# Hybrid decoder step: the feed-forward projections as two-by-two block products with seven products

## The chip, the cores and the metric

One core of a Trainium2 chip runs the whole program once. The metric is the device time of one execution in microseconds (us). TensorE multiplies, VectorE (DVE), ScalarE (ACT) and GpSimd (POOL) work on elements, SyncE (SP) only issues DMAs. SBUF is the on-chip memory with 128 partitions, PSUM has 8 banks into which TensorE writes, HBM is the memory outside.

## The reference

One layer of a decoder: a prompt of 1024 tokens and a sample group of 32 tokens share all weights, so T = 1056 columns. Three token mixers and their merge come first. The change touches what follows them:

```
x = x + (mixed @ w_out)
h2 = rmsnorm(x, norm2_w)
gu = h2 @ w_ffn_up                                   # 1024 -> 2 x 2816
x = x + (silu(gu[..., :D_FF]) * gu[..., D_FF:]) @ w_ffn_down   # 2816 -> 1024
y = rmsnorm(x, norm_f)                               # final norm
```

All in fp32.

## The kernel before

**Layout.** Activations lie with the feature on the partition and the token on the column: X1 is [128, 8, 1056], eight feature blocks (k = 0 to 7). The columns are cut in three chunks of 384, 384 and 288 (CHUNKS), because a PSUM bank holds 512 columns.

**Precision.** Each product of two fp32 numbers is made of three matmuls: every operand is split in a high part (rounded to fp32r) and a low part (the rest), and mm3 (lines 1277 to 1279) adds high weight x low data, low weight x high data and high weight x high data in PSUM. Each of the three has its own load of 128 x 128 weights.

**Weights.** A unit is 128 x 1024 weights, one output tile of a projection with depth 8 (or less for the down projection). SP loads it raw into WRAW (line 867), POOL loads it a second time into WH as the high part (the DMA into an fp32r tile, line 958) and subtracts to get the low part WL (line 961). There are two slots for each.

**FFN.** The 22 blocks of the inner width (2816 / 128) are cut in four passes of 6, 6, 5 and 5 blocks (FFN_PASSES). In a pass, each block needs two up tiles (gate and value). ACT takes Silu of the gate tile (line 2306), DVE multiplies (line 2355, FM), ACT casts the high part FH (line 2311) and DVE subtracts to the low part FL. FH and FL stay in SBUF. Then 8 down tiles of that pass, with depth 6 or 5, are added to X1 by DVE (add_to_x1). The loops over up and down tiles run in hardware loops on TensorE, SP and POOL. first_pair("up0") runs two up tiles interleaved, since it follows the norm's splitting chunk by chunk, and last_pair reorders the last two tiles of "out" and "down3" by chunk, so that the norm of a chunk can start early.

**Norms.** The norm ahead of the FFN (number 2) scales X1 into six small buffers HF5 (line 769), ACT casts them to HH (line 782), DVE and POOL subtract to HL (lines 755 and 1143). The final norm (number 3) works on single columns: TensorE sums the squares with a matmul of one column (lines 714 and 722), ACT takes the root and DVE the reciprocal of 2 or 3 columns (lines 676 and 702), TensorE spreads them (line 732), and DVE and POOL scale the rows, which SP and ACT store (lines 945 and 1844).

**Order.** Each engine runs its own instructions in the written order. Semaphores say what is ready: acc_done and acc_free for PSUM tiles, split_ok for weights, h_lo and f_lo for low parts. DMAs of one queue are also served in the order of issue.

## Time and profile before

| | us |
|---|---|
| median of three runs | 1761.59 (1761.56 to 1764.63) |
| span of the profiled execution | 1761.2 |
| TensorE busy | 1736.7 |
| DVE, ACT, POOL busy | 681.7, 384.9, 501.6 |
| FFN up to its last matmul, from the third up tile | 743.95 |

The profile is of one execution. A matmul's duration in it overlaps the next one's; the distance between two starts is what a matmul takes of the engine. PE is TensorE, PEld its weight loads. A time in a row's first column counts from the span's start. The shape of a matmul is rows x columns of the weights, then partitions x columns of the moving data.

### The profile page before, as it was taken

Reading aid. Unit: us, or ns where it says so; the run is one execution under the profiler, and the core shown is the slowest. Engines: PE = TensorE matmul, PEld = TensorE weight load, DVE = VectorE, ACT = ScalarE, POOL = GpSimd, SP = SyncE. Lnnn points to the kernel's source line nnn. Section 1 sums busy time; section 2 is a strip of 40 time slices with the busy share of each in tenths; the row PEclk is TensorE's granted clock in tenths of the full one; section 3 lists DMA queues with packets and bytes.
Section 4 is the critical chain, followed back from the end, with each engine's and each line's share of the span. In section 5 each row is a group of like instructions: output and inputs, shape, how many; then the busy total and the mean of one; then the engine's idle time right before and its main releaser. Section 6 shows DMA issues by size and latency. Waiting matters only on the chain.

```text
span 1761.2 us, 28504 instructions
## 1 busy us (share of the span) xinstructions
PE 1736.7 (99%) x11497; PEld 1689.1 (96%) x11497; DVE 681.7 (39%) x1406; ACT 384.9 (22%) x937; POOL 501.6 (28%) x504
## 2 busy tenths in 40 slices
PE   7999999999999999999999999999999999999998
PEld 7999999999999998898999999999999999999997
DVE  6859611318245537778732611110112111111125
ACT  5331121332123323534110411001110011001121
POOL 5482122223221211313223322222222222232222
PEclk9999999999999999999999999999999999999999
DMA  5454452332332345343642222233222322233224
GB/s 199 88 129 131 124 185 86 98 88 84 96 94 93 122 125 172 98 149 119 219 158 95 84 84 84 81 98 96 95 81 87 108 84 91 75 109 96 79 75 136
DMA packets 78384, 193.39 MB, mean 110 GB/s; under 512 B 13504, under 2 KB 33216, under 8 KB 78040
## 3 DMA queue, kind: packets, MB, share of 16 engines
q1 hardware_dynamic: 45616, 89.54, 16.7%
q0 software_dynamic: 20624, 66.10, 12.4%
q10 hardware_dynamic: 12056, 36.54, 6.0%
q8 instruction: 59, 0.97, 0.2%
q14 instruction: 29, 0.24, 0.0%
HBM read 167.45 MB, written 24.48 MB: 109 GB/s over the span
## 4 chain that ended last, share of the span: by engine, by line
PE 92%; DVE 4%; issue 1%; ACT 1%; DMA 1%; POOL 0%; SPq 0%; DVEq 0%; ACTq 0%; POOLq 0%
PE ps L1277 29%; PE ps L1278 28%; PE ps L1279 28%; PE ps L1707 1%; PE ps L1798 1%; PE ps L1477 1%; PE ps L1451 1%; ACT SB L2164 1%; PE ps L1771 0%; PE ps L1471 0%; PE ps L1652 0%; PE ps L1420 0%; DVE W_im L2355 0%; PE ps L1594 0%; DVE KTS L2355 0%
## 5 line engine op out<-in xcount | busy, mean ns | idle before, releaser
L1277 PE MATMUL ps<-HL,WH 128*128 128x384 f32 (+1 forms) x2496 | 819.0, 328 | 5.1 <-DVE HL L625 1.8
L1278 PE MATMUL ps<-HH,WL 128*128 128x384 f32 (+1 forms) x2496 | 807.0, 323 | 0.0
L1279 PE MATMUL ps<-HH,WH 128*128 128x384 f32 (+1 forms) x2496 | 805.9, 323 | 0.0
L1277 PEld LDWEIGHTS ps<-HL,WH 128*128 128x128 f32 x2496 | 469.5, 188 | 16.6 <-issue 9.3
L1278 PEld LDWEIGHTS ps<-HH,WL 128*128 128x128 f32 x2496 | 469.9, 188 | 0.3
L1279 PEld LDWEIGHTS ps<-HH,WH 128*128 128x128 f32 x2496 | 469.6, 188 | 0.0
L961 POOL TENSOR_TENSOR WL<-WRAW,WH 128x1024 fp32r<-128x1024 f32 (+2 forms) x131 | 295.0, 2252 | 449.3 <-DMA WH<-in_w 449.3
L958 POOL DMA_DIRECT2D WH<-in_w x131 | 75.5, 576 | 689.3 <-PE ps L1279 679.6
L2355 DVE TENSOR_TENSOR FM<-FS,ps 128x384 f32<-128x384 f32 (+1 forms) x66 | 34.3, 520 | 435.5 <-PE ps L1279 431.6
L1278 PE MATMUL ps<-FH,WL 128*128 128x384 f32 (+1 forms) x528 | 170.6, 323 | 0.0
L1277 PE MATMUL ps<-FL,WH 128*128 128x384 f32 (+1 forms) x528 | 169.9, 322 | 0.2 <-POOL WL L961 0.2
L1279 PE MATMUL ps<-FH,WH 128*128 128x384 f32 (+1 forms) x528 | 169.8, 322 | 0.0
L2355 DVE TENSOR_TENSOR X<-X,ps 128x384 f32<-128x384 f32 (+1 forms) x108 | 56.2, 521 | 233.3 <-PE ps L1279 233.3
L2306 ACT ACTIVATE FS<-ps 128x384 f32<-128x384 f32 (+1 forms) x66 | 30.6, 465 | 402.0 <-PE ps L1279 402.0
L1277 PEld LDWEIGHTS ps<-FL,WH 128*128 128x128 f32 x528 | 99.2, 188 | 0.5 <-POOL WL L961 0.5
L1279 PEld LDWEIGHTS ps<-FH,WH 128*128 128x128 f32 x528 | 99.2, 188 | 0.0
L1278 PEld LDWEIGHTS ps<-FH,WL 128*128 128x128 f32 x528 | 99.1, 188 | 0.0
L2311 ACT CAST FH<-FM 128x384 fp32r<-128x384 f32 (+1 forms) x66 | 31.9, 487 | 224.1 <-DVE FM L2355 224.1
L1867 ACT ACTIVATE GT<-ps 128x384 f32<-128x384 f32 (+1 forms) x72 | 33.3, 464 | 214.1 <-PE ps L1279 187.9
L2363 DVE SCALAR_TENSOR_TENSOR CV<-PX,CW,CV 128x120 f32<-128x120 f32 (+9 forms) x90 | 45.8, 575 | 0.6
L2363 DVE SCALAR_TENSOR_TENSOR PX<-PX,ps 128x384 f32<-128x384 f32 (+1 forms) x60 | 30.9, 517 | 23.0 <-PE ps L1279 16.0
L1853 ACT COPY PX<-ps 128x384 f32<-128x384 f32 (+1 forms) x36 | 16.3, 453 | 96.3 <-PE ps L1279 95.1
(361 smaller groups left out, 1610.7 us busy)
## 6 DMA issues: line engine op xcount, KB each, us to landing
WRAW<-in_w SPq DMA_DIRECT2D x111, 512.0 KB, 3.3
WH<-in_w POOLq DMA_DIRECT2D x102, 512.0 KB, 3.7
gate_scratch<-GT ACTq DMA_DIRECT2D x24, 528.0 KB, 3.2
PX<-gate_scratch ACTq DMA_DIRECT2D x22, 528.0 KB, 3.8
WRAW<-in_w SPq DMA_DIRECT2D x16, 384.0 KB, 3.0
WH<-in_w POOLq DMA_DIRECT2D x16, 384.0 KB, 3.3
WRAW<-in_w SPq DMA_DIRECT2D x16, 320.0 KB, 2.8
WH<-in_w POOLq DMA_DIRECT2D x16, 320.0 KB, 3.1
```

The lines of the kernel that those rows point to most:

```text
L958: nc.gpsimd.dma_start(WH[:, slot, 0:wd], src[:, 0:wd]).then_inc(s_high[slot], 16)
L961: nc.gpsimd.tensor_tensor(WL[:, slot, 0:wd], WRAW[:, slot, 0:wd], WH[:, slot, 0:wd].bitcast(F32), ALU.subtract).then_inc(split_ok, 1)
L1277: nc.tensor.matmul(out, wh, rl, start=start, stop=False)
L1278: nc.tensor.matmul(out, wl, rh, start=False, stop=False)
L1279: return nc.tensor.matmul(out, wh, rh, start=False, stop=stop)
L1451: last = nc.tensor.matmul(o[64 * e:64 * e + 64], STT[:, part, pr, 64 * e:64 * e + 64], U[:, 2 * pr + e, 0:SC], start=True, stop=True)
L1477: last = nc.tensor.matmul(o(i, e), off[r:r + 64, pr, :], HST[r:r + 64, part, 2 * half + i, :], start=False, stop=part == 1, skip_group_che ...
L1867: nc.scalar.activation(GT[:, c0:c0 + w], acc_of(no, n)[:, 0:w], ACT.Tanh, scale=0.5).then_inc(acc_free[n], 1)
L2306: nc.scalar.activation(FS[:, n, 0:w], acc[n][:, 0:w], ACT.Silu).then_inc(acc_free[n], 1)
L2311: nc.scalar.copy(FH[:, f, c0:c0 + w], FM[:, n, 0:w]).then_inc(f_hi, 1)
L2355: return nc.vector.tensor_tensor(out, a, b, op)
L2363: return nc.vector.scalar_tensor_tensor(out=out, in0=a, scalar=s, in1=b, op0=op0, op1=op1)
```

## The change

**The algorithm.** The moving data (h with 1024 features x 1056 tokens) is seen as two by two blocks: features 0 to 511 and 512 to 1023, tokens 0 to 527 (LOWER) and 528 to 1055 (UPPER). The weights of a pair of output tiles are also two by two blocks. Seven products of sums of blocks replace eight products of blocks. A product covers one block row of outputs: 128 outputs, half the tokens in two pieces of 264 columns (CHUNK), depth 4 in the up part. A group x is one pair of output tiles: seven products in the order 1, 5, 6, 7, 3, 2, 4. Their results are combined in PSUM and by DVE: products 6, 3 and 4 add onto the banks of products 1, 5 and 7 (QUAD, FRESH), after ACT has copied product 1 (R1) and then product 6 (R2) out; DVE adds quadrants from them.

**Up part.** The first block's two up tiles stay as they were. 21 groups (UP_PAIRS) do the other 42 tiles. Before the first, DVE forms four sums of h blocks in X1, in place, ACT casts their high parts and DVE subtracts the low parts; X1 itself has been stored in HBM (xscr), and the norm scales X1 in place where it used HF5. POOL forms four differences of weight blocks per group, in place in the raw weights, and seven low parts. The high parts of the weights are now copied by ACT, not loaded by DMA; a ring of six slots of 512 weights (RING) holds high and low.

**Between.** Of each pair of inner blocks, seven rows (four blocks' halves and three sums, high and low) are made by DVE and ACT and stored in HBM (fscr), ten pairs beside the up groups, the eleventh beside the first down groups.

**Down part.** Four stages over the inner width with 4, 6, 6 and 6 blocks (DOWN_TILES), depth 2, 3, 3, 3 in a product; each has four groups, one per pair of output tiles. SP loads each stage's rows from fscr and X1 back from xscr. DVE adds nine results per group to X1.

**Final norm.** Sums of squares, root and reciprocal are taken on the spread array, 128 partitions wide and 528 columns long, once for each half of the tokens.

All loops of the FFN are now written out. The core of the diff:

```diff
+HALF = T // 2
+CHUNK = HALF // 2
+UP_PAIRS = DFF // P - 1
+DOWN_TILES = [4, 6, 6, 6]
+PAIRS = UP_PAIRS + 4 * len(DOWN_TILES)
+ORDER, LAST_ORDER = (1, 5, 6, 7, 3, 2, 4), (1, 5, 6, 7, 4, 3, 2)
+QUAD = {1: 0, 6: 0, 5: 2, 3: 2, 7: 4, 4: 4, 2: 6}
+FRESH = (1, 5, 7, 2)
+RING = 6
...
# norm 2 on DVE: in place, behind the stores of X1
-            dve.scalar_tensor_tensor(m["hf"][i % slots][:, 0:w], m["src"](k)[:, c0:c0 + w], prm(m["weight"], k, 1),
+            if i == 0:
+                after(dve, s_x1s, 16 * LATE[0])
+            if k == LATE[0]:
+                after(dve, s_x1c[n], 16)
+            dve.scalar_tensor_tensor(m["src"](k)[:, c0:c0 + w], m["src"](k)[:, c0:c0 + w], prm(m["weight"], k, 1),
...
# POOL
+        for x in range(PAIRS):
+            after(pool, s_wr[x % 2], raw_loaded(x))
+            low(x, 0)
+            difference(x, W12, W11, W11, 1, 0)
+            difference(x, W22, W12, W12, 1, 1)
+            low(x, 1)
+            difference(x, W22, W11, W11, 2, 2)
+            low(x, 2)
+            difference(x, W21, W11, W11, 3, 3)
+            for i in range(3, 7):
+                low(x, i)
...
# TensorE
+            product, nk, g = order_of(x)[i], depth(x), 7 * x + i
+            bank_free(x, product)
+            after(pe, wl_ok, g + 1)
+            high, lo = ring(g)
+            for c in range(2):
+                out = quad(product)[:, c, :]
+                for k in range(nk):
+                    mh, ml = moving(x, product, k, c)
+                    wh, wl = high[:, k * P:(k + 1) * P], lo[:, k * P:(k + 1) * P]
+                    nc.tensor.matmul(out, wh, ml, start=product in FRESH and k == 0, stop=False, skip_group_check=True)
+                    nc.tensor.matmul(out, wl, mh, start=False, stop=False, skip_group_check=True)
+                    last = nc.tensor.matmul(out, wh, mh, start=False, stop=k == nk - 1, skip_group_check=True)
+            last.then_inc(pd.sem, 1)
...
# TensorE's waits in the first group (x = 0)
+                for n, tiles in {1: ((0, 1), (1, 1)), 5: ((2, 1), (0, 2)), 7: ((1, 2), (2, 2))}.get(product, ()):
+                    pe.wait_ge(acc_free[n], FFN_TILE + tiles)
+                if product == 6:
+                    after(pe, ar_used, 1)
...
# ACT, the first group (the norm's splitting stands just ahead)
+        weight_high(0)
+        first_silu(0)
+        h_sum_high(0)
+        weight_high(1)
+        first_silu(1)
+        h_sum_high(1)
+        weight_high(2)
+        weight_high(3)
+        h_sum_high(2)
+        first_silu(2)
+        for x in range(UP_PAIRS):
+            g, q = 7 * x, f_pair_beside(x)
+            if x >= 1:
+                silu(x - 1, RV, 5)
+            weight_high(g + 4)
+            if x == 0:
+                h_sum_high(3)
+            after(act, pd, done_count(x, 1))
...
+            nc.scalar.copy(by_chunk(R1), quad(1)).then_inc(ar_used.sem, 1)
...
# DVE, the first group
+        first_product(0)
+        h_sum(A22, A21, A22, ALU.add, 0)
+        h_sum_low(0)
+        first_product(1)
+        h_sum(A21, A11, A21, ALU.subtract, 1)
+        h_sum(A11, A22, A11, ALU.subtract, 2)
+        h_sum_low(1)
+        first_product(2)
+        h_sum_low(2)
+        h_sum(A12, A12, A11, ALU.subtract, 3)
+        h_sum_low(3)
...
# SP, last up group: x1_load and f_load are row loads of [128, 1056]
+                for s in range(STAGE):
+                    after(sp, s_fst[s], 16 * len(range(s, 70, STAGE)))
+                for j in range(2, 6):
+                    x1_load(j)
+                f_load(0, 0, done_count(x, 5))
+                f_load(0, 1)
+            raw_load(x + 2)
+            if x == UP_PAIRS - 1:
+                f_load(0, 2, done_count(x, 6))
+                f_load(0, 3)
+                f_load(0, 4, done_count(x, 7))
+                f_load(0, 5)
+                f_load(0, 6, done_count(x, 4))
...
# final norm on DVE
+            sums = quad((1, 7)[i])
+            dve.reciprocal(sums, sums).then_inc(frc.sem, 1)
```

## Rows read from the trace of the kernel before

**Rows 1.** The page: busy shares, granted clock, the chain that ended last.
```profile
PE 1736.7 (99%) x11497; PEld 1689.1 (96%) x11497; DVE 681.7 (39%) x1406; ACT 384.9 (22%) x937; POOL 501.6 (28%) x504
PE 92%; DVE 4%; issue 1%; ACT 1%; DMA 1%; POOL 0%; SPq 0%; DVEq 0%; ACTq 0%; POOLq 0%
```

**Rows 2.** Busy time by stretch (start:end, length, engines, clock, DMA share, GB/s).
```profile
1004.95:1748.90 743.95, 743.76 (x4630) 743.44 (x4629) 121.63 (x240) 74.48 (x147) 192.89 (x146) 1.00 0.28 88
```

**Rows 3.** Timeline of TensorE in an up tile: start, duration, line, operands, shape.
```profile
1205.12 0.34 PE L1278 MATMUL ps<-HH,WL 128*128 128x384 f32 x1
...
1210.04 0.34 PE L1279 MATMUL ps<-HH,WH 128*128 128x384 f32 x1
1210.21 0.29 PE L1277 MATMUL ps<-HL,WH 128*128 128x288 f32 x1
...
1211.94 0.29 PE L1278 MATMUL ps<-HH,WL 128*128 128x288 f32 x1
```

**Rows 4.** Timeline: loads and matmuls of few columns.
```profile
975.40 0.75 PEld L722 LDWEIGHTS ps<-PRM,AC 128*128 128x128 f32 x6
180.71 1.06 PEld L1471 LDWEIGHTS ps<-U,KTS 128*128 128x128 f32 x8
180.89 1.09 PE L1471 MATMUL ps<-U,KTS 128*128 128x137 f32 x8
```

**Rows 5.** Timeline from the norm's first scaling to the third up tile.
```profile
960.88 0.33 SPq L867 DMA_DIRECT2D WRAW<-in_w  x1
976.66 1.11 DVE L769 SCALAR_TENSOR_TENSOR FS<-X,PRM,ps 128x384 f32<-128x384 f32 x2
999.42 0.43 ACT L782 CAST HH<-FM 128x288 fp32r<-128x288 f32 x1 [0.36 <-DVE FM L769]
999.89 0.46 DVE L755 TENSOR_TENSOR HL<-FM,HH 128x288 fp32r<-128x288 f32 x1 [0.50 <-ACT HH L782]
1000.02 1.28 ACT L2306 ACT_TABLE_LOAD   x1 [0.16 <-POOL HL L1143]
1004.95 0.34 PE L1277 MATMUL ps<-HL,WH 128*128 128x384 f32 x1
```

**Rows 6.** Groups by form (count, busy us, mean ns), and one timeline row.
```profile
L2355 DVE TENSOR_TENSOR FL<-FM,FH 128x384 fp32r<-128x384 f32 x44 | 22.4, 551 | 0.0
L522 DVE TENSOR_TENSOR AC<-AC,GT 128x1056 f32<-128x1056 f32 x6 | 7.5, 1254 | 0.2
1213.98 1.39 DVE L2355 TENSOR_TENSOR FL<-FM,FH 128x384 fp32r<-128x384 f32 x3
L1898 ACT CAST WH<-WRAW 128x512 fp32r<-128x512 f32 x4 | 2.3, 611 | 0.5 <-DMA WRAW<-in_w 0.5
L1172 POOL TENSOR_TENSOR WL<-WRAW,WH 128x512 fp32r<-128x512 f32 x4 | 4.9, 1275 | 0.0
L986 POOL TENSOR_TENSOR HST<-BC,SP 128x256 f32<-128x256 f32 x4 | 2.7, 696 | 0.1
```

**Rows 7.** Timeline of TensorE after its idle start.
```profile
17.36 0.69 PE L1277 MATMUL ps<-HL,WH 128*128 128x384 f32 x1 [1.81 <-DVE HL L625]
22.65 0.41 PE L1278 MATMUL ps<-HH,WL 128*128 128x384 f32 x1
```

**Rows 8.** A stretch with busy DMAs; a DMA issue (KB, us to landing).
```profile
4.00:24.00 20.00, 13.40 (x52) 12.09 (x53) 12.81 (x25) 13.43 (x29) 15.25 (x22) 1.00 1.05 385
WRAW<-in_w SPq DMA_DIRECT2D x111, 512.0 KB, 3.3
```

**Rows 9.** Timeline of the end.
```profile
1748.64 0.29 PE L1279 MATMUL ps<-FH,WH 128*128 128x288 f32 x1
1752.56 4.71 DVE L2363 SCALAR_TENSOR_TENSOR X<-X,PRM,ps 128x384 f32<-128x384 f32 x10
```

**Rows 10.** Reciprocals by form.
```profile
L2389 DVE RECIPROCAL SP<-SP 128x16 f32<-128x16 f32 x1 | 0.2, 221 | 0.0
L340 DVE RECIPROCAL DTT<-DTT 128x72 f32<-128x72 f32 x1 | 0.6, 603 | 0.0
```

More of the change, by code:

```diff
@@ new lines, in _, with final_sum @@
+        for x in range(PAIRS - 1):
+            for i in range(7):
+                strassen_product(x, i)
+        def final_sum(product, half, squares, start, stop):
+            for c in range(2):
+                last = nc.tensor.matmul(quad(product)[:, c, :], prm("ones"), by_chunk(squares[:, half])[:, c, :], start=start,
+                                        stop=stop, skip_group_check=True)
+            return last
+        for i in range(6):
+            strassen_product(PAIRS - 1, i)
@@ new lines, in _, with quadrant @@
+        first_product(0)
[9 more added lines that the diff above has]
+        h_sum_low(3)
+        def quadrant(x, out, held, product, turn):
+            after(dve, pd, done_count(x, product))
+            tt(by_chunk(out), by_chunk(held), quad(product), ALU.add).then_inc(dr.sem, 1)
```

649 lines of the change are left out of this document (509 added, 140 removed).

## The prediction

> **What bounds the kernel now.** The page's busy shares come first: TensorE is busy for 1736.7 of 1761.2 us, DVE, ACT and POOL for under half, and the chain that ended last lies on TensorE for 92% [rows 1]. The stretches of the feed-forward part (FFN) come second: from its third up tile to its last matmul there are 743.95 us, TensorE is busy for 743.76 of them, the granted clock is 1.00 (the 2.4 GHz level), DVE and POOL have 122 and 193 us of work and the DMAs run at 88 GB/s [rows 2]. So here a matmul less is time less, until another engine or a transfer is late. Third is the timeline: what a matmul costs is the distance of two starts, not its duration of 0.34 us, which overlaps. 28 steps of 384 columns take 4.92 us (175.7 ns each), 13 steps of 288 columns 1.73 us (133.1 ns) [rows 3]. An up tile is 48 of the first and 24 of the second, 11.63 us; the waits between tiles cost nothing.
>
> **The matmuls.** The first up pair stays. Before, the other 42 up tiles and the 8 x 22 down steps take the 743.95 us. After, each of 21 pairs is 7 products x 2 halves x 4 steps x 3 = 168 matmuls, and the down part 4 x 7 x 2 x 3 x 11 = 1848 (11 is the sum of the depths 2, 3, 3, 3): 5376 matmuls of 264 columns. Columns fall by one eighth, which at before's rate would be 93 us. But no matmul of 264 columns with full weights is in the trace. From 288 to 384 columns a start costs 0.444 ns per column more, and the line gives 133.1 - 24 x 0.444 = 122.4 ns at 264. The other side is the weight load, one per matmul as before: six loads with one-column matmuls take 0.75 us, (0.75 - 0.19)/5 = 112 ns each, and eight with 137 columns (1.06 - 0.19)/7 = 124 ns by the loads, (1.09 - 0.28)/7 = 116 ns by the matmuls [rows 4]. The ends are thus 112 ns (only the load binds) and 133 ns (no fall below the 288 step); if the step bends between 137 and 288 columns, the chord gives 116 + 127/151 x 17 = 130 ns. I take 123 ns, the line, rounded up: 264 columns are nearest to the 288 row and the load still fits. 5376 x 0.123 = 661.2 us; the small matmuls among the last tiles (four groups of six, each near the 0.7 us of [rows 4]) give way to one of about 0.25 us. The stretch becomes 661.5 us: **-82.5 us**.
>
> The Trainium skill, page "TensorE: Matmul & The Clock Gate", section "Back-to-back issue gap", gives N/2.4 + 2.5 ns for an isolated warm matmul. By it, an estimate, a step of 264 columns is 112.5 ns and the matmuls 605 us, 56 us less than my term; but at 288 it says 122.5 where this trace has 133.1, and at 384 it says 162.5 where the trace has 175.7, so I go by the trace.
>
> **The start of the block products.** Before, DVE and ACT end the norm's splitting at 1000.3 and 999.85, and TensorE goes from the first pair to the next at 1004.95 without a gap [rows 5]. After, the new operands (four sums of 4 half-rows, their high and low parts) must be made in this gap. A half-row is 528 wide. DVE: 384 take 551 ns, 1056 take 1254, so 528 about 0.70, in a queue 0.08 less (three, with 384, 384 and 288 columns, in 1.39 us), 0.62. ACT: a 512-wide weight copy takes 0.61, so 528 about 0.63; from PSUM I take 0.6 [rows 6]. I follow the written order. ACT: weight copy to 1000.5, table load 1.28, Silu to 1002.3. DVE then has three products of 0.5 and 28 half-row operations up to the fourth sum, 1.5 + 17.4 us, plus 2.6 waiting for the third Silu, which on ACT stands behind the second and third sums' casts and two weight copies: 1002.3 + 21.5 = 1023.8, with hand-overs 1024.4. ACT casts that sum (0.63) and only then copies product 1 out of PSUM, to 1025.6. Product 6 accumulates on those banks and waits for it. Product 1 itself waits for the second Silu (1007.5), product 5 for the third (1018.3). Unhindered product 6 would start at 1004.95 + 2 x 2.95 = 1010.85. Loss 14.7 us. TensorE is idle for 4, 8 and 4 us in it. After its idle start it runs 384 columns at 0.32 us a step for 5.3 us, the 1.2 GHz level by the step, before it goes to 0.175 [rows 7]: 16 steps, 2.3 us lost; this comes on top once. **+17 us**, between 10 (sums overlap better) and 24.
>
> **The norm ahead of it.** It now overwrites X1 in place and so waits for X1's stores. SP can issue them from 960.9, behind its weight load: 5.3 MB with the first group's raw weights, at 380 GB/s 14 us, landed at about 976.5; the first scaling is at 976.66 [rows 5]. **+1**, between 0 and 3.
>
> **Steady up groups.** One is 168 x 0.123 = 20.7 us. POOL has 7 lows and 4 differences of 512 columns, 11 x 1.275 = 14.0 us; ACT in the fuller of two groups 7 weight copies, 2 bank copies, 2 Silus, 7 casts, about 11.1 us; DVE 5 quadrants, 2 products, 4 sums, 7 lows, 18 x 0.62 = 11.2 us [rows 6]. None is a bound. Their hand-overs hide as long as product 1's copy is made within 5.9 us of the group's start: by the order DVE ends the old group 3 us into the new, ACT copies at about 5.2. Cover gone, each 0.1 us costs 2.1 us. In the first down stage a group is 84 x 0.123 = 10.3 us and POOL has 11 operations of 256 columns at 0.70, 7.7 us, DVE up to 15 operations, 9.3 us. I take **+2**, between 0 and 30.
>
> **Transfers.** A stored row pair is 128 x 1056 x 4 = 541 KB. Saturated, this trace moved 385 GB/s over 20 us; a 512 KB load lands 3.3 us after its issue [rows 8]. So 1.4 us per row and 1.5 to 2 behind it. The last up group (0 to 20.7) can start them late: X1's loads at 2.5, four f loads after product 5 (5.9), four after 6, four after 7, two at the end, with 0.5 MB of weights between: 19 transfers, served one behind the other to about 31. The first down group wants the row of its fifth product at 26.5, the last at 29.5: about 3 us late in sum. The next stage wants 21 loads (11.4 MB); they start only when the last stores have landed, some 28 us into the first down stage, and end about 5 us after the product that wants them. Stages three and four: 15 loads and weights within 28.8 us, served in 24, on time. Sum 8 at 385 GB/s; at 320 the same walk gives 22. I take **+10**, between 3 and 22. What hides the rest is the 20 us of each stage's last group.
>
> **The tail.** Before, the last FFN matmul starts at 1748.64, the last row operation ends at 1757.27, the end is 1761.2: 12.3 us after the matmuls [rows 9]. After, the root is taken on the spread sums, 528 wide, and its reciprocal on DVE. A reciprocal of 16 elements takes 221 ns, of 72 603 [rows 10]: 6.8 ns an element, so 528 cost 0.6 + 456 x 0.0068 = 3.7 us, twice. DVE from the last product's end: reciprocal to 3.7, copy and a row to 5.25, the last add to 5.95, four rows to 8.7, second reciprocal to 12.45, seven rows at 0.68 to 17.5 (after the spread copy), then 3.9 us of stores as before: 21.4. **+9**; if a wide reciprocal costs only what an add does (0.7), +2.
>
> The Trainium skill, page "VectorE: DVE Perf Modes", section "First, the fixed hardware budget", says that Reciprocal is an iterative divide with a repeat count of 8; at the add's 1.05 ns an element that would be, an estimate, 4.4 us for 528, and the rows at 6.8 ns agree in kind. By it the tail would be +10.5.
>
> **Sum.** 1761.2 - 82.5 + 17 + 1 + 2 + 10 + 9 = 1717.7 for the profiled execution; the median shown, 1761.59, lies 0.4 above its span: **1718 us**.
>
> **Rivals.** (a) The waits hide: sums and transfers cost half of my 28 us or less, 1700 down to 1690. For it: the first sums are independent of each other; against: the in-order ACT queue. (b) The hand-overs of ACT, POOL and DVE are late in every group, 1.5 us in 21 groups: 1718 + 31 = 1749. For it: 18 DVE and 18 ACT operations cross each other; against: each engine has half of its time free [rows 2]. (c) The step bends, 130 ns: +38, 1756. (d) **Slower than before:** a matmul with its own full load does not come below the 288 step, 133.3 ns. The price is 5376 x 10.3 ns = 55 us, 1773. It decides above 123 + 43.5/5.376 = 131 ns. For it: the 288 step exceeds its pure columns by 13 ns, and the 137-column step by 59; against: the 112 ns loads. (e) The step falls to the load's 112 ns: -59, 1659; against it the excess of 13 to 16 ns at both sizes. (f) The block products save no columns after all: as (d) or above.
>
> **Chances.** Forecast 0.50 (own range 1700 to 1738), (a) 0.17, (b) 0.15, (c) 0.07, (d) with (f) 0.07, (e) 0.04. A measurement of this kernel can tell 0.2%, 3.5 us, from no change. Faster: all but (d), (f) and a part of (c): 0.90; the same 0.03; slower 0.07. The range, to leave out no more than two in ten: 1690 to 1750.
>
> **What would show it.** TensorE starts 0.123 us apart in steady groups, 20.7 us per group; three gaps of TensorE right after 1005 us, the last ending on the ACT copy of product 1; gaps in the first down group and at the start of the second stage that end on DMAs; two DVE reciprocals near 3.7 us in the tail; a part after the last product of 21 us. A step above 130 ns, or ends of idle time on POOL in every group, would make the prediction wrong.

## The result and the profile after

The changed kernel takes 1742.27 us (median of 4 runs, 1741.4 to 1743.63), the kernel before 1761.84 (1761.56 to 1764.63) on the same chip: ratio 0.9884, 95% interval 0.9870 to 0.9898. The forecast was 1718 us, so the gain is 19.6 us where 43.6 were expected; the stated range (1690 to 1750) holds the time, the forecast's own (1700 to 1738) doesn't. The profiled execution has a span of 1740.7 us.

The page of the changed kernel, its part on busy time and the chain that ended last, answers to [rows 1]:

```profile
PE 1660.2 (95%) x12229; PEld 1605.7 (92%) x12229; DVE 951.8 (55%) x1615; ACT 557.6 (32%) x1239; POOL 797.6 (46%) x761
...
PE 75%; DVE 8%; POOL 7%; issue 4%; ACT 4%; DMA 2%; SPq 0%; ACTq 0%; DVEq 0%; POOLq 0%
```

TensorE lost 76.5 us of work and the span only 20.5; a quarter of the chain has left TensorE, where before it was 8%. The busy time by stretch of the changed kernel shows where (start:end, length, then PE, PEld, DVE, ACT, POOL busy, granted clock, DMA share, GB/s), and answers to [rows 2]. The stretches are the first up group of block products (group 0), groups 1 to 20, the first down stage (groups 21 to 24), the first two groups of the second stage (25 and 26), groups 27 to 35, the last group (36), and what follows its last product:

```profile
1013.10:1051.00 37.90, 24.51 (x168) 24.12 (x169) 24.80 (x33) 13.96 (x25) 22.12 (x16) 0.77 0.09 29
1051.00:1471.10 420.10, 410.60 (x3362) 408.51 (x3361) 234.53 (x251) 161.68 (x290) 303.77 (x221) 1.00 0.43 151
1471.10:1521.70 50.60, 42.77 (x339) 41.41 (x338) 34.70 (x48) 15.50 (x37) 34.23 (x43) 1.00 0.87 328
1521.70:1562.30 40.60, 33.06 (x254) 32.34 (x253) 12.31 (x18) 7.14 (x15) 25.32 (x26) 0.96 0.80 312
1562.30:1700.70 138.40, 138.40 (x1137) 138.21 (x1136) 60.73 (x84) 37.92 (x69) 100.39 (x100) 1.00 0.50 187
1700.70:1720.40 19.70, 16.62 (x131) 16.09 (x130) 11.63 (x15) 7.00 (x10) 2.94 (x3) 1.00 0.00 1
1720.40:1740.70 20.30, 3.34 (x11) 1.90 (x9) 14.65 (x15) 2.52 (x4) 5.12 (x4) 0.61 0.56 213
```

Only the fifth stretch has TensorE busy throughout, at 0.122 us a step. The undisturbed up groups (1, 3, 5, ...) take 20.4 us, 0.1214 us a step; the timeline of TensorE in the changed kernel, start and duration of each, shows the steps (seventeen of them between the two lines shown, 2.05 us), answering to [rows 3]:

```profile
1120.83 0.28 PE L2144 MATMUL ps<-SOP,WH 128*128 128x264 f32 x1
...
1122.88 0.29 PE L2146 MATMUL ps<-SOP,WH 128*128 128x264 f32 x1
```

The idle times of TensorE in the changed kernel's timeline, with what ended them in brackets, in the order of the stretches: three in group 0, one of the ten in groups 2, 4, ... 20 (all alike), five in group 21, four in group 25, one in group 36:

```profile
1013.15 0.36 PE L2144 MATMUL ps<-HL,WH 128*128 128x264 f32 x1 [3.25 <-issue]
...
1025.29 0.59 PE L2144 MATMUL ps<-SOP,WH 128*128 128x264 f32 x1 [8.97 <-ACT FS L2648]
...
1034.34 0.59 PE L2144 MATMUL ps<-SOP,WL 128*128 128x264 f32 x1 [4.37 <-ACT RB L2696]
...
1078.35 0.39 PE L2144 MATMUL ps<-SOP,RINGB 128*128 128x264 f32 x1 [0.92 <-ACT RB L2696]
...
1476.21 0.36 PE L2144 MATMUL ps<-SOP,RINGB 128*128 128x264 f32 x1 [1.99 <-issue]
...
1486.66 0.36 PE L2144 MATMUL ps<-HL,WL 128*128 128x264 f32 x1 [0.81 <-DVE X L2789]
...
1529.29 0.36 PE L2144 MATMUL ps<-HL,RINGB 128*128 128x264 f32 x1 [0.92 <-DVE X L2789]
...
1543.19 0.36 PE L2144 MATMUL ps<-SOP,WH 128*128 128x264 f32 x1 [3.41 <-issue]
...
1712.57 0.39 PE L2144 MATMUL ps<-HH,RINGB 128*128 128x264 f32 x1 [2.90 <-DVE X L2789]
```

The account against the forecast, each from the starts of the groups; the nominal length of a group is its number of matmuls times 0.1215 us (20.4, 10.2 and 15.3 us):

| part | forecast | measured | how |
|---|---|---|---|
| matmuls | -82.5 | -90.8 | 5376 x 0.1215 = 653.2 against 743.95 |
| later start | +1 | +4.8 | products possible at 1009.7, before at 1004.95 |
| group 0 | +17 | +20.9 | 1051.0 - 1009.7 - 20.4 |
| up groups 1 to 20 | +2 (with the down part's hand-overs) | +12.1 | 420.1 - 408.0 |
| first down stage | +10 for all transfers | +9.8 | 50.6 - 40.8 |
| second down stage | in that | +10.1 | 71.37 - 61.24, group 25 alone 24.9 |
| stages 3 and 4 | 0 | +0.5 | |
| last group | 0 | +4.4 | 19.7 - 15.3 |
| behind the last product | +9 | +8.0 | 20.3 - 12.3 |

The sum is -20.2 for a span that fell by 20.5.

### The profile page after: what moved, and what is told of

Same layout as the page of the kernel before. It is cut to its first block, busy times and chain, and to the rows that moved or that the text cites. A ratio compares the mean times of both kernels' runs of the same rounds, so it can differ in the third digit from the quotient of the medians.

```text
span 1740.7 us, 30849 instructions
## 1 busy us (share of the span) xinstructions
PE 1660.2 (95%) x12229; PEld 1605.7 (92%) x12229; DVE 951.8 (55%) x1615; ACT 557.6 (32%) x1239; POOL 797.6 (46%) x761
## 4 chain that ended last, share of the span: by engine, by line
PE 75%; DVE 8%; POOL 7%; issue 4%; ACT 4%; DMA 2%; SPq 0%; ACTq 0%; DVEq 0%; POOLq 0%
PE ps L1559 14%; PE ps L1560 13%; PE ps L1561 13%; PE ps L2144 9%; PE ps L2146 9%; PE ps L2145 9%; POOL RAWB L1249 4%; DVE X L2789 1%; POOL WL L1249 1%; DMA x_scratch<-X 1%; POOL RINGB L1249 1%; POOL WH L1249 1%; ACT STG L2669 1%; PE ps L1989 1%; PE ps L2080 1%
## 5 line engine op out<-in xcount | busy, mean ns | idle before, releaser
L1559 PE MATMUL ps<-HL,WH 128*128 128x384 f32 x1488 | 492.3, 331 | 5.3 <-DVE HL L685 1.8
L1560 PE MATMUL ps<-HH,WL 128*128 128x384 f32 x1488 | 481.7, 324 | 0.0
L1561 PE MATMUL ps<-HH,WH 128*128 128x384 f32 x1488 | 481.1, 323 | 0.0
L1559 PEld LDWEIGHTS ps<-HL,WH 128*128 128x128 f32 x1488 | 280.6, 189 | 16.7 <-issue 9.3
L1560 PEld LDWEIGHTS ps<-HH,WL 128*128 128x128 f32 x1488 | 280.8, 189 | 0.3
L1561 PEld LDWEIGHTS ps<-HH,WH 128*128 128x128 f32 x1488 | 280.5, 188 | 0.0
L1224 POOL TENSOR_TENSOR WL<-WRAW,WH 128x1024 fp32r<-128x1024 f32 x59 | 145.1, 2459 | 233.8 <-DMA WH<-in_w 233.8
L2789 DVE TENSOR_TENSOR X<-X,ps 128x528 f32<-128x528 f32 (+1 forms) x162 | 107.2, 681 | 177.0 <-PE ps L2146 126.1
L2145 PE MATMUL ps<-HH,WL 128*128 128x264 f32 x292 | 83.1, 285 | 0.0
L2146 PE MATMUL ps<-HH,WL 128*128 128x264 f32 x292 | 83.0, 284 | 0.0
L2145 PE MATMUL ps<-HH,RINGB 128*128 128x264 f32 x292 | 82.9, 284 | 0.0
L2146 PE MATMUL ps<-HH,RINGB 128*128 128x264 f32 x292 | 82.8, 284 | 0.0
```

The costliest lines, as they stand in the source:

```text
L1224: nc.gpsimd.tensor_tensor(WL[:, slot, 0:wd], WRAW[:, slot, 0:wd], WH[:, slot, 0:wd].bitcast(F32), ALU.subtract).then_inc(split_ok, 1)
L1559: nc.tensor.matmul(out, wh, rl, start=start, stop=False)
L1560: nc.tensor.matmul(out, wl, rh, start=False, stop=False)
L1561: return nc.tensor.matmul(out, wh, rh, start=False, stop=stop)
L2145: nc.tensor.matmul(out, wl, mh, start=False, stop=False, skip_group_check=True)
L2146: last = nc.tensor.matmul(out, wh, mh, start=False, stop=k == nk - 1, skip_group_check=True)
```

## The experiments

Theories: *order*: on ScalarE's in-order queue the copy of product 1 (R1) stands behind a Silu that waits for VectorE, and similar places on the other queues make the rest. *Port*: VectorE and GpSimd slow each other, and this makes VectorE late. *Volume*: in the down part the bytes bind, not their order. The ratio given is always against the kernel before on the same chip; the changed kernel's is 0.9884. The kernel before took 1761.8 to 1763.8 us on the five chips of these runs, so medians of different kernels are compared to about 2 us. Single traces scatter too: the norm's second reciprocal, on which no edit below but norm_raw_late's can act, lies between 975.4 and 978.3 us. Where a trace is compared by place, the text says from which point.

**r1_early.** In even up groups ScalarE copies R1 ahead of the Silu of the group before.

```diff
-            if x >= 1:
+            late_silu = x >= 2 and x % 2 == 0
+            if x >= 1 and not late_silu:
                 silu(x - 1, RV, 5)
...
             nc.scalar.copy(by_chunk(R1), quad(1)).then_inc(ar_used.sem, 1)
+            if late_silu:
+                silu(x - 1, RV, 5)
```

> In every second up group the copy of product 1's banks (R1) now stands ahead of the Silu of the group before on ACT. Theory 'order': the 0.95 us gap of TensorE at product 6 of groups 2, 4, ... 20 is there only because that copy stands behind a Silu that waits for DVE's last quadrant. Then all ten gaps go, the groups of 21.6 us fall to 20.4, and the time falls by 10 to 12 us (1742.3 to about 1731), although DVE's slow operations stay slow. Rival 'engines full': DVE and POOL together are late by themselves; the gap moves to the next wait of the same groups (product 3 or 7) and the time falls by less than 3 us.

Measured: 1731.03 us, ratio 0.9817 (0.9801 to 0.9833), 11 us below the changed kernel. ScalarE in the same place of group 2, first in the changed kernel:

```profile
1076.64 0.65 ACT L2674 ACTIVATE RB<-RB 128x528 f32<-128x528 f32 x1 [2.06 <-DVE RB L2789]
1077.19 0.60 ACT L2643 CAST WH<-RAWB 128x512 fp32r<-128x512 f32 x1
1077.70 0.59 ACT L2696 COPY RB<-ps 128x528 f32<-128x528 f32 x1
```

then with the copy early:

```profile
1074.93 0.59 ACT L2697 COPY RB<-ps 128x528 f32<-128x528 f32 x1
1076.57 0.65 ACT L2674 ACTIVATE RB<-RB 128x528 f32<-128x528 f32 x1 [1.05 <-DVE RB L2792]
```

and the busy time of groups 1 to 20 of the kernel with the copy early (columns as above):

```profile
1050.90:1458.80 407.90, 407.90 (x3362) 407.90 (x3361) 235.56 (x251) 161.69 (x290) 308.68 (x221) 1.00 0.44 155
```

The Silu waits 2.06 us for VectorE and the copy behind it ends at 1078.29, just before the product that waited (1078.35). With the order turned, TensorE is busy for all of 407.9 us: the 12.1 us of the up groups are gone. Group 21 takes 1.3 us of it back, waiting longer for transfers.

**tiny_diffs.** GpSimd forms the four differences of raw weight blocks per group on 4 of each block's 128 columns, so the products use wrong weights; everything else is as in the change.

```diff
-            tt(raw_part(x, *out), raw_part(x, *a), raw_part(x, *b), ALU.subtract)
+            tt(raw_part(x, *out)[:, :, 0:4], raw_part(x, *a)[:, :, 0:4], raw_part(x, *b)[:, :, 0:4], ALU.subtract)
```

> POOL's four weight differences of each group are made on 4 of 128 columns per block only, so the products work on wrong weights; everything else is as it was. It takes some 4 us of POOL out of each up group. Theory 'port': DVE's operations with both operands in SBUF (0.70 us alone, 1.7 us in the trace beside a POOL operation) are slow because POOL works at the same time, and this is what makes the chain late. Then the sums of the first group take 0.7 us each less often 1.0 to 1.4, the first group's loss falls from 21 us by 3 to 5 us, the gaps at product 6 of every second group go, and the time falls by 15 to 20 us. Rival 'order' alone (ACT's in-order queue, POOL's differences not involved): the gaps at product 6 stay at 0.95 us and the time falls by less than 3 us.

Measured: 1722.6 us, ratio 0.9772 (0.9756 to 0.9789), 20 us below the changed kernel. Every up group takes 20.4 us although the order on ScalarE is untouched (R1's copy is made 3.6 us into group 2 instead of 6.3), and group 1 starts at 1044.4 instead of 1051.0. Of these 6.6 us, 2.8 are there before product 0 is possible (1006.9 for 1009.7), where other kernels with unchanged code scatter as much; from that point to group 1 it is 37.5 us against 41.3, so 3.8 are the edit's. So the up groups' loss needed both: the order, and a Silu that is late.

What made it late is followed back from R1's copy of group 2: ScalarE in the changed kernel, which waits for GpSimd's difference, and VectorE behind it:

```profile
1069.70 0.62 ACT L2643 CAST RINGB<-RAWB 128x512 fp32r<-128x512 f32 x1 [3.64 <-POOL RAWB L1249]
...
1070.89 1.36 DVE L2789 TENSOR_TENSOR STG<-FODD,STG 128x528 fp32r<-128x528 f32 x1 [3.20 <-ACT STG L2669]
...
1074.62 1.38 DVE L2789 TENSOR_TENSOR STG<-FODD,STG 128x528 fp32r<-128x528 f32 x1 [0.34 <-ACT STG L2669]
```

the same two engines in tiny_diffs, and its busy time of groups 1 to 20:

```profile
1060.32 0.62 ACT L2644 CAST RINGB<-RAWB 128x512 fp32r<-128x512 f32 x1 [1.23 <-POOL RAWB L1249]
...
1061.50 1.38 DVE L2790 TENSOR_TENSOR STG<-FODD,STG 128x528 fp32r<-128x528 f32 x1 [0.76 <-ACT STG L2670]
```

```profile
1044.38:1452.30 407.92, 407.92 (x3362) 407.92 (x3361) 228.82 (x250) 162.74 (x290) 215.82 (x221) 1.00 0.44 158
```

The cast of weights (RINGB) stands on ScalarE's queue ahead of the cast (STG) that VectorE waits for, and itself waits for GpSimd. It starts 18.67 us into group 1 in the changed kernel and 15.94 in tiny_diffs: 2.7 us earlier, and R1's copy is 2.7 us earlier too. So in the up groups the edit acts through GpSimd's time and ScalarE's order. It hardly acts through slow operations of VectorE: those stay (1.38 us where 0.70 is usual, in both kernels), and VectorE's busy time falls by 6 us in 20 groups, GpSimd's by 88.

Slow operations there are all the same. The changed kernel's timeline shows them when the rows of GpSimd (POOL) and VectorE (DVE) are laid side by side:

```profile
1061.78 1.30 POOL L1249 TENSOR_TENSOR WL<-RAWB,WL 128x512 fp32r<-128x512 f32 x1 [2.85 <-ACT WL L2643]
...
1061.85 1.79 DVE L2789 TENSOR_TENSOR STG<-GT,STG 128x528 fp32r<-128x528 f32 x1
...
1084.20 2.73 POOL L1249 TENSOR_TENSOR WRAW<-WRAW 128x512 f32<-128x512 f32 x2
...
1084.59 0.70 DVE L2789 TENSOR_TENSOR FODD<-RB,ps 128x528 f32<-128x528 f32 x1 [1.67 <-PE ps L2146]
...
1091.73 0.71 DVE L2789 TENSOR_TENSOR FODD<-FODD,RB 128x528 f32<-128x528 f32 x1 [0.71 <-ACT RB L2674]
...
1091.74 1.84 POOL L1249 TENSOR_TENSOR WRAW<-WRAW 128x512 f32<-128x512 f32 x1
```

At 1061.85 VectorE starts an operation on two SBUF operands 0.07 us behind GpSimd's; GpSimd's ends at 1063.08, VectorE's at 1063.64, 0.56 later. At 1091.73 VectorE was first, keeps its 0.71, and GpSimd takes 1.84 where 1.30 is usual. At 1084.59 one operand is in PSUM (ps) and nothing is slowed. So the two don't share, by these rows: the later one waits for about the end of the earlier. The Trainium skill says this, page "SBUF — State Buffer", section "Who interferes with whom": a VectorE instruction with two SBUF inputs contends with a GpSimd instruction that reads SBUF, as an exclusive lock, and one with a single SBUF input (outside the two-port modes) doesn't. This trace agrees, with 0.70 us against 1.79. What this lock costs the up groups by itself no run separates from GpSimd's time (which holds what the lock adds to GpSimd's own operations): the two VectorE operations on the path to R1's copy lose 1.3 us by it (1.36 and 1.38 for 0.70), about as much as the copy is late, and both run slow in tiny_diffs as well, which has no gap. Before, GpSimd was busy for 193 of 744 us in this part [rows 2]; now it is for 304 of 420.

**first_order.** ScalarE's order in group 0: all three Silus as early as they can, R1's copy ahead of the casts of the fourth sum.

```diff
         first_silu(0)
+        first_silu(1)
         h_sum_high(0)
+        first_silu(2)
         weight_high(1)
-        first_silu(1)
         h_sum_high(1)
...
         h_sum_high(2)
-        first_silu(2)
...
-            if x == 0:
-                h_sum_high(3)
...
             nc.scalar.copy(by_chunk(R1), quad(1)).then_inc(ar_used.sem, 1)
+            if x == 0:
+                h_sum_high(3)
```

> In the first group ACT does the second Silu ahead of the first sum's casts, the third behind them, and copies product 1 ahead of the fourth sum's casts. Theory 'order': products 1, 5 and 6 of the first group wait for things that ACT could have done earlier; product 5 starts when its sum is ready (1015 us in place of 1025), product 6 when the second sum's low parts are (about 1024 in place of 1034), product 3 at about 1034 on the fourth sum. First group 37.9 us to about 30, time -7 to -9 us. Rival 'DVE': the sums and low parts on DVE (32 operations, 26 us in the trace) set the end of the group whatever ACT does: -2 us or less.

Measured: 1737.86 us, ratio 0.9853 (0.9836 to 0.9869), 4.4 us below the changed kernel. Group 1 starts at 1042.7, 8.3 us earlier than in the changed kernel. Of that, 2.1 us lie ahead of the edit's place (product 0 is possible at 1007.6 for 1009.7); from there to group 1 it is 35.1 us against 41.3, so the edit has 6.2, a little less than expected, and all_seven and four_edits below have the same 35.1 and 35.0. Groups 1, 2, 25 and 26 give back 2.1 us. Another 2.3 come back in the last group, at a place that the edit doesn't touch. Busy time there, in this kernel and then in the changed one, just behind the idle time of 2.9 us that both have (length, PE, PEld, DVE, ACT, POOL, clock):

```profile
1708.00:1710.00 2.00, 2.00 (x11) 2.00 (x11) 0.00 (x0) 0.00 (x0) 0.00 (x0) 0.50 0.00 0
```

```profile
1712.60:1714.60 2.00, 2.00 (x16) 2.00 (x17) 0.71 (x1) 0.64 (x1) 0.00 (x0) 1.00 0.00 0
```

Behind the same idle time TensorE is granted 1.2 GHz (0.50) for 6 us in one kernel, steps of 0.22 us, and stays at 2.4 GHz in the other; 27 slow steps cost 2.7 us. Of the kernels told of here, r1_early, norm_raw_late, x1_late, f13_early and thin_tail have slow steps at this place too; those with the edit of last_sums, whose idle time is 0.8 us, have none. The changed kernel, tiny_diffs and raw_first kept the level behind the same idle time. What decides it I can't say; it is a part of the scatter.

**norm_raw_late.** The load of group 0's raw weights (1 MB) is issued behind the stores of X1 that the norm waits for, not ahead of them.

```diff
-        sp.wait_ge(mx_lo, 16)
-        raw_load(0)
         for k in range(LATE[0]):
...
+        raw_load(0)
         sp.wait_ge(split_ok, FFN + 2)
```

> SP issues the 1 MB load of the first group's raw weights behind the stores of X1 in place of ahead of them. Theory: the first scaling of the norm waits 3.2 us for those stores, because 5.3 MB are in the queues from 963 on at 409 GB/s; with 1 MB less ahead of them they land 2.6 us earlier, and all that follows too: -2.5 us. Rival: the load of the second up unit's high weights on the other queue (landed 8 us after its wait began, used by a subtraction at 978.8) is what holds the first pair; it gains little from the order of SP's queue: 0 to -1 us.

Measured: 1741.45 us, ratio 0.9873 (0.9856 to 0.9889); the median can't be told from the changed kernel's. The trace can: VectorE's first scaling of the norm, in the changed kernel and then in this one:

```profile
981.56 1.14 DVE L816 SCALAR_TENSOR_TENSOR X<-X,PRM,ps 128x384 f32<-128x384 f32 x2 [3.17 <-DMA x_scratch<-X]
```

```profile
978.29 1.13 DVE L816 SCALAR_TENSOR_TENSOR X<-X,PRM,ps 128x384 f32<-128x384 f32 x2
```

The wait for X1's stores is gone. From the norm's second reciprocal to the point where product 0 is possible it is 29.6 us against 31.5. In the five kernels with this edit this distance is 29.6 to 29.8, in the ten others, the changed kernel among them, 31.3 to 32.0: the edit gives 2 us, as its theory has it, a little less than the 2.5 expected. Where product 0 starts doesn't show it (1011.2 here, 1010.6 to 1011.4 in the four kernels below without the edit), because the point before scatters by more.

**x1_late.** The rereads of the residual (four of 541 KB) stand behind the loads of the first down stage's activations.

```diff
-                for j in range(2, 6):
-                    x1_load(j)
                 f_load(0, 0, done_count(x, 5))
...
                 f_load(0, 6, done_count(x, 4))
+                for j in range(2, 6):
+                    x1_load(j)
```

> The 8 rereads of the residual for the first four blocks of rows are issued behind the loads of the down stage's first activations, not ahead of them. In the trace of the changed kernel the first down group (x = 21) takes 17.1 us where its 84 steps of 0.1215 us are 10.2, with five gaps of 0.8 to 2.0 us in front of products 2 to 6 that end on transfers; groups 22 and 23 take 11.6 each. If the order on the queue is the cause (theory queue order): x = 21 falls to 11 to 13 us, the next two groups keep theirs, and the kernel gains 4 to 6 us on the changed kernel's 1742.3, about 1737. If the transfers are bound by their sum and not their order (theory volume): what x = 21 gains comes back as a wait for the residual in groups 22 to 25, and the time stays within 1.5 us of 1742.3.

Measured: 1738.22 us, ratio 0.9858 (0.9842 to 0.9875). Group 21 falls from 17.1 to 11.2 us, as the order theory has it; groups 22 and 23 take 24.2 together (23.2 before), and groups 25 and 26 take 41.5, against 40.7 in the changed kernel and 38.6 to 38.8 in last_sums and thin_tail, which don't touch this part. A wait that comes in their place is for the residual, VectorE's and behind it TensorE's (the timeline of x1_late):

```profile
1483.57 1.32 DVE L2789 TENSOR_TENSOR X<-X,ps 128x528 f32<-128x528 f32 x2 [1.62 <-DMA X<-x_scratch]
...
1484.33 0.39 PE L2144 MATMUL ps<-SOP,WH 128*128 128x264 f32 x1 [1.15 <-DVE X L2789]
```

Both theories are right in part: 4.9 us gained in the first stage (50.6 to 45.7). What is given back in the second, this run alone doesn't show, as first_order, whose edit lies elsewhere, has 41.4 us there too. The pairs that differ in the edit do below: 37.2 us with it and 34.6 without (all_seven, four_edits; the first has norm_raw_late too), 35.9 and 35.0 (all_raw, six_raw).

**f13_early.** One row pair of the second stage's activations (i = 3) is loaded at x = 21, not behind the wait for the last part's stores. (The expectation says two parts and four loads; the edit moves this one part.)

```diff
+            if (d, m) == (0, 0):
+                f_load(1, 3, done_count(UP_PAIRS - 1, 4))
...
-                for i in range(4):
+                for i in range(3):
```

> The four loads of activations for the second down stage's last two parts are issued at x = 21 ahead of the others instead of behind the wait for the last part's store. In the changed kernel's trace x = 25 takes 24.9 us against 15.3 nominal, its gaps of 0.9, 1.5, 1.7 and 3.4 us behind transfers. Theory queue order: these gaps shrink to 2 us together, gain 3 to 5 us, about 1738. Theory volume (about 400 GB/s is all the queues give from 1475 to 1545): the bytes come ahead of others that x = 21 to 24 want, those gaps grow by as much, and the time is within 1.5 us of 1742.3 or slower.

Measured: 1738.4 us, ratio 0.9856 (0.9839 to 0.9872). Groups 25 and 26 take 37.7 us against 38.8 and 38.6 in the two kernels below and 40.7 in the changed one; the first three gaps of group 25 (0.9, 1.5 and 1.7 us) are down to one of 0.5, the last, 3.4 us, stays. A gain of 1 us is in the trace beyond what the neighbours have without the edit; the rest of the 4 us of the median is not its.

**last_sums.** The two sums of squares stand between the first and the second addition of the last groups.

```diff
             down_add(x, m, 0, 0, 1)
+            if d == 3 and m >= 2:
+                for j in range(2):
+                    after(dve, fad, 2 * m - 3 + j)
+                    square_sum(slice(0, T), (SQ5, GT)[j], 2 * m - 1 + j)
             down_add(x, m, 1, 1, 5)
```

(and taken away from where they stood behind it)

> In the last down groups VectorE forms the two sums of squares between the first and the second addition to the residual, not ahead of both. In the changed kernel's trace the last group's fifth product starts 2.9 us late behind VectorE's addition, which stands behind two sums of 1.3 us each. Theory: that wait falls by the 2.6 us of the two sums and the kernel gains 2 to 4 us, about 1739. Rival (the tail, not the hand-over, sets the end): the sums are wanted by the final norm just as late, and the time stays within 1 us of 1742.3.

Measured: 1738.28 us, ratio 0.9863 (0.9847 to 0.9880), span of the profiled execution 1732.8. The changed kernel's VectorE ahead of the fifth product of group 36 (started 1712.57), and this kernel's TensorE at the same product:

```profile
1709.36 1.25 DVE L2789 TENSOR_TENSOR AC<-AC,SQ 128x1056 f32<-128x1056 f32 x1
1710.64 1.26 DVE L2789 TENSOR_TENSOR AC<-AC,GT 128x1056 f32<-128x1056 f32 x1
1711.82 0.69 DVE L2789 TENSOR_TENSOR X<-X,ps 128x528 f32<-128x528 f32 x1
```

```profile
1704.65 0.70 DVE L2789 TENSOR_TENSOR X<-X,ps 128x528 f32<-128x528 f32 x1 [0.27 <-PE ps L2146]
```

In the changed kernel the addition stands behind 2.5 us of sums; here it waits only for TensorE's product, and the fifth product starts 3.2 us behind the fourth instead of 5.3 (2.2 without a wait). The idle time of TensorE falls from 2.9 to 0.8 us, and the steps behind it stay at 0.12 us. From the start of group 36 to the end it is 37.2 us against 40.0: 2.8 gained; the rest of what the span fell lies ahead of the edit.

**thin_tail.** The final norm's sums, roots and reciprocals on 88 partitions by 6 columns, spread to all rows by six small matmuls.

```diff
-            dve.reciprocal(sums, sums).then_inc(frc.sem, 1)
+            dve.reciprocal(thin_root(i), thin_root(i)).then_inc(frc.sem, 1)
...
+                last = nc.tensor.matmul(quad((1, 7)[i])[:, j // 3, TOK * (j % 3):TOK * (j % 3) + TOK],
+                                        bc(RC2[0:TOK, 2 + 6 * i + j:3 + 6 * i + j], [TOK, P]), IDENT[0:TOK, 0:TOK], ...)
```

> The final norm's sums, roots and reciprocals are formed with 88 tokens on the partitions and 6 in a row, and spread to all rows by TensorE, in place of two reciprocals of 528 elements on every partition. In the changed kernel's trace each of these took 3.46 us and stood on the path at the end. Theory: the two reciprocals fall to about 0.2 us each, small matmuls and one more hand-over each add about 0.7 us, and of the gain of 2.8 us on each only the part on the path counts: 3 to 6 us, about 1738. Rival (the row scalings and the stores behind them bound the tail): 0 to 1.5 us gained.

Measured: 1736.69 us, ratio 0.9854 (0.9837 to 0.9870). VectorE's two forms, of the changed kernel and then of this one:

```profile
1719.31 3.46 DVE L3389 RECIPROCAL ps<-ps 128x528 f32<-128x528 f32 x1
...
1728.41 3.46 DVE L3389 RECIPROCAL ps<-ps 128x528 f32<-128x528 f32 x1 [0.91 <-ACT ps L2757]
```

```profile
1715.95 0.18 DVE L3409 RECIPROCAL RC<-RC 88x6 f32<-88x6 f32 x1
```

From the last product's start to the end it is 18.4 us, against 22.5 in the changed kernel: 4.1 gained, in the expected range.

**all_seven, four_edits, all_tiny.** The seven edits r1_early, first_order, norm_raw_late, x1_late, f13_early, last_sums and thin_tail together; the same without norm_raw_late and x1_late; and the seven with tiny_diffs (wrong weights again). Their diffs are those above.

> All seven edits of the runs before together: the copy of R1 ahead of the Silu in even up groups, the first group's order on ScalarE, the weights' load behind the X1 stores, the rereads of the residual late, two down loads early, the last sums between the additions, and the final norm on 6 columns. If the seven act on different waits (theory sum), their single gains of 11.2, 4.4, 0.8, 4.1, 3.9, 4.0 and 5.6 us on the changed kernel's median add up to 34 us: about 1708. If the down stage's transfers are bound by their sum (theory volume), what the up groups save comes back in groups 21 to 25, whose bytes cannot come earlier: the 8.5 us of the two load edits and a part of the 16 us saved ahead of them are lost, 1714 to 1722. My value is 1709.

> As all_seven, but the load of the first raw weights and the rereads of the residual stay where the change has them: R1's copy, the first group's order, two down loads early, the last sums and the thin final norm. In the trace with the rereads late, groups 21 to 24 got 4.3 us shorter and groups 25 and 26 some 3 us longer, so theory volume expects the two kernels within 2 us of each other, theory sum expects this one 4 to 5 us slower than all_seven (about 1713).

(four_edits holds five of the seven edits.)

> all_seven with GpSimd's differences of weight blocks formed on 4 of each block's 128 columns (the products then use wrong weights). Alone, this took 19.7 us off, as VectorE's sums no longer stand behind GpSimd's and the first group began 6.6 us earlier. If the order on ScalarE was what turned the shared time of VectorE and GpSimd into a wait of TensorE (theory order), the 12 us of the even up groups are already gone in all_seven and only the first group's part remains: 4 to 7 us faster than all_seven. If the slowing itself costs TensorE time in other ways (theory port), 10 us or more.

Measured: all_seven 1709.15 us (5 runs, 1708.48 to 1709.8), ratio 0.9695 (0.9682 to 0.9709); four_edits 1712.71, ratio 0.9717 (0.9704 to 0.9731); all_tiny 1702.44, ratio 0.9658 (0.9645 to 0.9672). all_seven is faster than both kernels, by 53.6 us and by 33 us. Its stretches (the columns as above: group 0, groups 1 to 20, 21 to 24, 25 and 26):

```profile
1006.80:1041.80 35.00, 23.53 (x170) 22.94 (x169) 28.27 (x37) 14.77 (x27) 20.36 (x13) 0.85 0.09 31
1041.80:1450.50 408.70, 408.25 (x3362) 408.05 (x3361) 237.71 (x251) 163.28 (x293) 312.05 (x223) 1.00 0.44 155
1450.50:1497.60 47.10, 42.48 (x338) 41.26 (x337) 33.83 (x48) 15.05 (x37) 33.90 (x43) 1.00 0.99 389
1497.60:1534.80 37.20, 32.70 (x255) 32.33 (x254) 12.31 (x18) 7.20 (x15) 25.39 (x26) 0.95 0.78 302
```

The single gains add up in the raw medians (34 us expected, 33.1 measured). As ratios, which take out the chip, they sum to 0.0214 and all_seven has 0.0189 (some 38 and 33 us), and by place they don't add up either: in the first down stage the DMAs are now busy for 0.99 of the time at 389 GB/s, so little is left to gain there by order. Groups 21 to 26 take 84.3 us in all_seven and 85.2 in four_edits, so of the 3.6 us between the two the rereads' order has 0.9; product 0 of group 0 starts 3.3 us earlier, of which 2.2 are norm_raw_late's edit (from the second reciprocal on) and 1.1 lie ahead of it. And all_tiny is 6.7 us faster than all_seven, 8.0 by the spans of the two traces: 3.5 from the point where product 0 is possible to group 1 (35.1 to 31.6), 0.7 in group 1, 3.1 in groups 21 to 24, 0.9 given back in 25 and 26, and 1.6 ahead of group 0, which is scatter. With the order mended, GpSimd's differences cost nothing in groups 2 to 20, as theory order says, but they still cost in group 0 and in the first down stage.

**raw_first, all_raw, six_raw.** What TensorE waits for at the end of group 25 is told by ScalarE and SP's queue in the changed kernel's timeline:

```profile
1522.60 3.49 SPq L1104 DMA_DIRECT2D RAWB<-in_w  x2
...
1539.22 0.51 ACT L2643 CAST WL<-RAWB 128x384 fp32r<-128x384 f32 x1 [14.67 <-DMA RAWB<-in_w]
```

The weights of group 26 are issued at 1522.6, behind six loads of activations, and land 16.6 us later. So in raw_first their load goes ahead of those six; all_raw is all_seven with this, six_raw is all_raw without x1_late.

```diff
+            if x + 2 < PAIRS:
+                raw_load(x + 2)
             if (d, m) == (0, 3):
                 f_load(1, 4, done_count(x, ORDER[1]))
                 f_load(1, 5, done_count(x, ORDER[2]))
-            if x + 2 < PAIRS:
-                raw_load(x + 2)
```

> The changed kernel, but the raw weights of group 26 are loaded ahead of the activations of parts 4 and 5 of the second down stage, not behind their six loads. In the changed kernel's trace this load is issued at 1522.6, ScalarE waits 14.7 us for it until 1539.2, and with the differences behind it products wait until 1543.2 and 1546.6. Theory order: the load is issued some 8 us earlier, the last gap of group 25 (3.4 us) and the gaps up to group 26 (1.2 us) go, the activations come about 2.5 us later: 2 to 4 us gained on 1742.3, about 1739, and ScalarE's wait is shorter by 6 us or more. Theory volume: the gap in front of the products that want parts 4 and 5 grows by what the other loses, and the time stays within 1.5 us.

> all_seven with this edit too. Its groups 25 and 26 take 37.2 us for 30.6 nominal. Theory order: 33 to 35 us and 1706 to 1707 us in all. Theory volume (the DMAs were busy for 0.99 of the first down stage): no gain, 1709.

> As all_raw, but with the rereads of the residual where the change has them. The rereads' order was worth 0.9 us between all_seven and four_edits in the trace. Theory order expects group 21 near 17 us again and this kernel 1 to 4 us slower than all_raw; theory volume expects the two within 1 us.

Measured: raw_first 1740.29 us, ratio 0.9870 (0.9855 to 0.9885); all_raw 1706.55 (1705.75 to 1707.43), ratio 0.9677 (0.9664 to 0.9690); six_raw 1710.62, ratio 0.9701 (0.9687 to 0.9714). ScalarE at the same weights in raw_first:

```profile
1528.87 0.51 ACT L2643 CAST WL<-RAWB 128x384 fp32r<-128x384 f32 x1 [6.21 <-DMA RAWB<-in_w]
```

The wait falls from 14.7 to 6.2 us. Groups 25 and 26 take 38.6 us instead of 40.7, which is also what last_sums and thin_tail have without the edit, and the fifth product of group 25 starts 6.2 us behind the fourth, not 3.9: alone, the wait changes its place, as theory volume says, and the ratio can't be told from the changed kernel's. In all_raw the two groups take 35.9 us against all_seven's 37.2, and the median is 2.6 us lower. Groups 21 to 26 take 82.5 us in all_raw and 86.1 in six_raw, so with this edit the late rereads are worth 3.5 us. all_raw is the fastest kernel of all, 36 us below the changed one.

## Why the prediction was wrong

**Matmuls: right in kind, better in size.** The step is 0.1215 us, on the line that was drawn through 288 and 384 columns (122.4 ns); no bend, no floor at the 288 step. Rivals (c), (d), (e) and (f) fall.

**The step that failed is "Steady up groups ... None is a bound ... I take +2".** The forecast has R1's copy at about 5.2 us into the group, 0.7 us ahead of its need at 5.9. In even groups it is made at 6.3 (1077.70, the group's start being 1071.4) and ends at 6.9: 1.2 us late in each of ten groups, 12.1 us. That is rival (b)'s mechanism at 0.4 of its price. The link that was wrong is "DVE ends the old group 3 us into the new": its last quadrant ends at 5.2 (1076.61). The forecast compared each engine's sum of work with the 20.7 us of a group (14.0 for GpSimd) and did not walk ScalarE's queue, on which a cast that VectorE needs stands behind one that waits 3.6 us for GpSimd's difference. tiny_diffs takes the time of the differences away, and the copy comes at 3.6 us; r1_early shows that the copy's place in the queue made it TensorE's loss. The second thing missing is that VectorE's work was priced at durations read where GpSimd stood still, 0.62 to 0.70 us, while the change adds work to both engines on SBUF operands: 1.3 us of slowed operations lie on the same path. Whether the copy would have been late without these, or only by these, no run shows.

**The second step that failed: "Sum 8 at 385 GB/s ... I take +10".** 10 us were forecast for transfers and 20 are there; the walk was half of it. The rate of 385 GB/s was right (389 at most over a stage), and the places too (group 21, group 25). The walk had the rereads of the residual and the weights among its bytes, but it let the first down group be late from its fifth product on, 3 us in sum, where the trace has 6.9 us in front of five products, the third to the last (moving the rereads behind takes 5.9 us off that group, by x1_late). And it counted the weights of group 26 as bytes alone: they stand behind the activations and, once landed, still need a cast and GpSimd's differences, 4 us from 1539.2 to 1543.2. x1_late and raw_first each brought a wait at another place, and all_seven has the DMAs busy for 0.99 of the first stage: bytes bind as well. Groups 21 to 26, nominally 71.4 us, take 91.2 in the changed kernel and 82.5 in all_raw; as the traces without an edit of the loads have 88.4 to 91.6 there, the order of the queue recovers 6 to 9 us of the 20.

**The last group: not foreseen.** 4.4 us, of which 2.9 are one wait of the fifth product behind two sums of squares. The forecast took the order there as before.

**First group, norm and tail.** +20.9 for +17: the gaps were foreseen as three (4, 8 and 4 us, measured 3.3, 9.0 and 4.4) with the last on R1's copy (L2696), and so it is; the steps at 1.2 GHz behind the second and third cost about 3.7 us for 2.3. VectorE needs 26 us for 32 half-row operations there where 0.62 each give 20, and by tiny_diffs and all_tiny GpSimd's differences have 3.5 to 3.8 us of the start of group 1; here the sums themselves get shorter (3.90 to 2.56 us for the first four). The norm had +4.8 for +1: 1.7 of it was already there before the norm's sums (a load at 972.63 that before ran at 970.97), which is within the scatter of the traces, and 3.1 came after, with the wait of 3.2 us for X1's stores; issuing group 0's raw weights behind those stores takes the wait away and gives 2 us back in all five kernels that have it. The tail is right: 20.3 us for 21.4, reciprocals 3.46 us for 3.7.

The terms missed by -8.3 (matmuls), +3.8 (start), +3.9 (group 0), +10.1 (up groups), +9.9 (transfers), +0.5, +4.4 (last group) and -1.0 (tail): together 23.3 us, and 23.0 lie between the forecast's 1717.7 for the profiled execution and the span of 1740.7.

**Open:** what lets the granted clock fall behind the idle time of 2.9 us in some kernels and not in others; what the slowing of VectorE beside GpSimd costs by itself, apart from GpSimd's own time; and whether the down part's bytes can be cut, which no run tried.

## What to carry to other kernels

When a change takes work off the bound engine and gives it to others, an engine's sum of work below the length of a group doesn't make it harmless. Walk the in-order queues: a cast that waits for a third engine holds up all that stands behind it, and a copy that frees a bank belongs ahead of it. Moving this copy gave 11 us, and eight small edits of order and form 36, more than the change itself. Price operations as they run beside each other, not alone: here those of VectorE with two SBUF operands went from 0.70 to as much as 1.8 us. Where the DMAs are near their rate, follow every load of the queue, the weights too.

## What the runs showed of the hardware

- VectorE's operations with two SBUF operands and GpSimd's don't overlap: the later one ends 0.56 us behind the earlier one's end (VectorE), or takes 1.84 for 1.30 us (GpSimd); with a PSUM operand on VectorE's side nothing is slowed (0.70).
- A step of 264 columns with its own full load is 0.1215 us, within 1 ns of the line through 133.1 ns at 288 and 175.7 at 384 [rows 3].
- A reciprocal of 128x528 takes 3.46 us, of 88x6 0.18; with 0.22 for 16 and 0.60 for 72 in a row [rows 10] that is 6.3 to 6.8 ns for each element of a row.
- Behind 2.9 us of idle time at 2.4 GHz the level was kept in the traces of three kernels and fell to 1.2 GHz, for up to 6 us, in those of six others.
